# The recurrent passes stream both parts of x through one matmul of 512 columns, and the weights' rounding moves ahead of the gates

## The chip, the cores and the metric

The kernel runs on one core of a Trainium2 chip. The metric is the device time of one execution in microseconds; for the kernel before it is 1924.56, the median of three runs (1923.87 to 1925.30). The profiled execution took 1924.1 us by the same clock; its span, from the first to the last instruction of the trace, is 1922.0 us.

## The reference

The program computes three layers on x of 256 tokens by 2048 features, in fp32. The first layer holds the part that the change touches: RMS norm, one wide projection `z = xn @ w_in`, then a recurrent branch, an attention branch and gates. Cut to the recurrent branch:

```
xn = rms_norm(x, norm_pre_w)
u_lru, g_lru, ... = split(xn @ w_in)                 # 2048 features each
u = centred_depthwise_conv(u_lru, conv_w, conv_b)    # four taps along the tokens
for each direction (forward, backward):
    gate_r = sigmoid(u @ w_r + b_r); gate_i = sigmoid(u @ w_i + b_i)   # 16 blocks of 128
    a = exp(-8 * gate_r * softplus(-lam))
    h += scan over the tokens of  a * h + sqrt(1 - a*a) * (gate_i * u)
y_a = h * silu(g_lru)
```

Attention, the merging of both branches and two further layers of another kind follow; the change leaves them alone but for the value of some semaphore waits.

## The kernel before

**Slots.** All weights are cut into slots of 128 x 2048 fp32 values (1 MB) and pass through a ring of five places. For each slot SyncE issues a DMA (line 267) as soon as the slot five before it is used up; ScalarE rounds it to fp32r (`w_hi`, `Ring.round`, line 273); VectorE writes the remainder (`w_lo`, `Ring.residual`, line 281); TensorE then multiplies. x is split in the same way, into `xn_hi` and `xn_lo`, which lie side by side in one tile `xn`. A product is w_hi x_hi + w_hi x_lo + w_lo x_hi.

**Two ways to multiply a slot of features.** `Ring.features` (line 299) loads a 128 x 128 weight tile and streams 256 columns, three times for each of 16 tiles of the contraction, all into the same 256 columns of a PSUM bank: 48 matmuls per slot (line 308). `Ring.halves` (line 311) sends w_hi once against both parts of x as 512 columns and w_lo against x_hi as 256, so 32 matmuls per slot (lines 319 and 320); the sum then lies in two halves of the bank, and someone has to add them. The attention part of the kernel uses `halves` already, and there VectorE adds with a `tensor_reduce` (line 946).

**Passes.** The recurrent branch takes eight passes i of two feature tiles each (b = 0, 1). A pass has four slots: 4i and 4i+1 give u (banks z[0], z[1]), 4i+2 and 4i+3 give the gate g (banks z[2], z[3]). Then TensorE does 16 plain fp32 matmuls for the recurrent gates (`gates`, line 1126), which need the convolved u of this pass. TensorE runs its own instruction list pass by pass; each of the four slots waits until its bank was read out in the pass before.

**ScalarE and VectorE.** Both run a written-out order in nine iterations i (lines 616 to 644 and 880 to 910). Iteration i does the input side of pass i (copy of u out of PSUM, convolution) and the output side of pass i-1 (gates, decays, scan, y), and between these pieces the rounding and the remainder of slots n+3 to n+6, n = 4i. No engine reorders its list. In order, in the kernel before:

- ScalarE: sigmoid of g read from PSUM (`gate_inputs`, line 572), eight gate sigmoids (580, 582), round(n+3), four tanh (592), round(n+4), two copies of u into `padded` (610), four exp (599), a square root (602), round(n+5), round(n+6), rounding of y (614).
- VectorE: g times its sigmoid (`open_gates`, 850), residual(n+3), residual(n+4), two convolutions (839, 843), scan (856 to 865), residual(n+5), sum of directions and y (870, 873), residual(n+6), remainder of y (877).
- GpSimd multiplies gate_i by u (524).

In iteration 0 VectorE computes a softplus chain at the end (lines 912 to 917), and in iteration 2 a chain for the rotary tables (366 to 375), between y and residual(n+6). After the last pass come four slots for the keys (32 to 35, `tokens`, line 332) and four for the values (36 to 39); after slot 37 TensorE transposes the keys (1167), for which VectorE has rotated them (924 to 930).

Of the kernel before, what the change touches and what calls it, by code (L numbers as in the profile page):

```python
# [12 lines left out]
ACT = mybir.ActivationFunctionType  # L13
ALU = mybir.AluOpType
AX_X = mybir.AxisListType.X
# [3 lines left out]
T = 256  # L19
# [13 lines left out]
LRU_PASSES = KT // 2  # L33
# [326 lines left out]
def reduce_angles(link, dve, angle, turns, rest, looked):  # L360
# [4 lines left out]
    for n, quarter in enumerate((0.0, 0.25)):  # L365
# [5 lines left out]
        for m, part in enumerate(turn_parts):  # L371
# [3 lines left out]
        link(lambda: dve.tensor_scalar(rest, rest, -3.1415925, None, ALU.max))  # L375


B1_SEMS = ("loaded0 loaded1 loaded2 loaded3 loaded4 rounded split used "
           "p1_in ident_in consts_in x0 x1 x2 x3 eps squared averaged rooted first0 first1 first2 first_rounded first_split second_rounded second_split scaled ascaled turned xrounded xsplit "
           "weights0 weights1 gated cleared chain exped ucopied conv gsig zcopied gates taken decay dsteps rounded_y ydone "  # L380
           "counted rotary_in rchain rlooked mask_in sink_in sinkready "
# [6 lines left out]
def first_parts(k, t, s):  # L388

    nc = k.nc  # L390
    z, aux = k.z, k.aux
# [65 lines left out]
    def tile(n):  # L457
        return z[n][:, 0:T]
# [67 lines left out]
    def scalar(act):  # L526
# [38 lines left out]
        ring.round(act, 2)  # L565

        def gate_inputs(i):
            act.wait_ge(s.used, 4 * i + 4)
            if i:
                act.wait_ge(s.zcopied, 2 * i)  # L570
            for b in range(2):
                act.activation(gsig[:, b], tile(2 + b), ACT.Sigmoid).then_inc(s.gsig, 1)

        def gates(i):
            if i:
# [28 lines left out]
        def input_copy(i, b):  # L604
            act.wait_ge(s.used, 4 * i + b + 1)
            if i:
                act.wait_ge(s.conv, 8 * (i - 1) + 4 * b + 4)
            else:
                act.wait_ge(s.cleared, 1)
            act.activation(padded[:, b, 2:2 + T], tile(b), ACT.Copy).then_inc(s.ucopied, 1)  # L610

        def round_y(i):
            act.wait_ge(s.dsteps, 8 * i + 8)
# [1 line left out]

        for i in range(LRU_PASSES + 1):
            n = 4 * i
            if i:
                gate_inputs(i - 1)
                gates(i - 1)  # L620
            ring.round(act, n + 3)
            if i:
                tanhs(i - 1)
            ring.round(act, n + 4)
            if i < LRU_PASSES:
                input_copy(i, 0)
                input_copy(i, 1)
            if i:
                exps_lru(i - 1)
            else:  # L630
                act.wait_ge(s.chain, 2)
                act.activation(tmp[1][:], tmp[0][:], ACT.Exp).then_inc(s.exped, 1)
            ring.round(act, n + 5)
            if i == 2:

                act.wait_ge(s.rchain, RCHAIN_1 + 8)
                act.activation(sin_1[:, :, 0:16], rest_1[:, :, 0:16], ACT.Sin, scale=-1.0).then_inc(s.rlooked, 1)
                act.activation(sin_1[:, :, 16:32], rest_1[:, :, 16:32], ACT.Sin).then_inc(s.rlooked, 1)
            ring.round(act, n + 6)
            if i == 2:  # L640
                act.wait_ge(s.rchain, RCHAIN_1 + 16)
                act.activation(cos_1[:], rest_1[:], ACT.Sin).then_inc(s.rlooked, 1)
            if i:
                round_y(i - 1)
# [29 lines left out]
            act.activation(yb_hi[:, 4 * c + 2 * p:4 * c + 2 * p + 2], y_now[p][:], ACT.Copy).then_inc(yrounded[p], 1)  # L674

        def silu(c, j):
            act.wait_ge(s.zcopied, 2 * LRU_PASSES + 4 * c + j + 1)
            act.activation(gate[:, j], gate[:, j], ACT.Silu).then_inc(s.silued, 1)

        def finish_chunk(c, n):  # L680
# [102 lines left out]
    def vector(dve):  # L783
# [46 lines left out]
               .then_inc(s.second_split if q < 3 else s.split, 1)  # L830
        ring.residual(dve, 2)

        def convolve(i, b):
            dve.wait_ge(s.ucopied, 2 * i + b + 1)
            u = u_all[:, 2 * i + b:2 * i + b + 1]
            for tap in range(4):
                x = padded[:, b, tap:tap + T]
                if tap == 0:
                    ins = dve.tensor_scalar(u, x[:, None], col(P1_CONV, 2 * i + b), col(P1_CONVB, 2 * i + b),
                                            ALU.mult, ALU.add)  # L840
                else:
                    dve.wait_ge(s.conv, 8 * i + 4 * b + tap)
                    ins = dve.scalar_tensor_tensor(out=u, in0=x[:, None], scalar=col(P1_CONV + 16 * tap, 2 * i + b),
                                                   in1=u, op0=ALU.mult, op1=ALU.add)
                ins.then_inc(s.conv, 1)

        def open_gates(i):
            dve.wait_ge(s.gsig, 2 * i + 2)
            for b in range(2):
                dve.tensor_tensor(g_all[:, b], tile(2 + b), gsig[:, b], ALU.mult).then_inc(s.zcopied, 1)  # L850

        def scan(i):
            def step(n):
# [14 lines left out]
        def outputs_lru(i):  # L868
            dve.wait_ge(s.dsteps, 8 * i + 6)
            dve.tensor_tensor(gate_r[:, :, 0], gate_r[:, :, 0], gate_r[:, :, 1], ALU.add).then_inc(s.dsteps, 1)  # L870
            dve.wait_ge(s.zcopied, 2 * i + 2)
            dve.wait_ge(s.dsteps, 8 * i + 7)
            dve.tensor_tensor(y[:], gate_r[:, :, 0], g_all[:], ALU.mult).then_inc(s.dsteps, 1)

# [4 lines left out]

        for i in range(LRU_PASSES + 1):  # L880
            n = 4 * i
            if i:
                open_gates(i - 1)
            ring.residual(dve, n + 3)
            if i == 0:
                link = chain(dve, s.chain)
                link(lambda: dve.tensor_scalar(rate[:], params[:, P1_LAM:P1_LAM + 32], -1.0, None, ALU.mult))
                link(lambda: dve.tensor_tensor(tmp[0][:], rate[:], params[:, P1_LAM:P1_LAM + 32], ALU.min))
            ring.residual(dve, n + 4)
            if i < LRU_PASSES:  # L890
                convolve(i, 0)
                convolve(i, 1)
            if i:
                scan(i - 1)
            if i == 2:
                rlink = chain(dve, s.rchain)
                dve.wait_ge(s.counted, 1)
                dve.wait_ge(s.rotary_in, 16)
                rlink(lambda: dve.tensor_copy(angle_1[:], pos_1[:]))
                for m in range(2):  # L900
                    rlink(lambda: dve.tensor_tensor(angle_1[:, m], angle_1[:, m], rotary[:], ALU.mult))
            ring.residual(dve, n + 5)
            if i:
                outputs_lru(i - 1)
            if i == 2:
                reduce_angles(rlink, dve, angle_1[:], turns_1[:], rest_1[:], (s.rlooked, 2))
            ring.residual(dve, n + 6)
            if i:
                split_y(i - 1)
            else:  # L910
                dve.wait_ge(s.exped, 1)
                softplus_tail(link, dve, rate[:], tmp[1][:], tmp[0][:], tmp[2][:])
                link(lambda: dve.tensor_scalar(scale_a[:], rate[:], -8.0, None, ALU.mult))
                link(lambda: dve.tensor_scalar(scale_t[:], rate[:], 4.0, None, ALU.mult))
                dve.wait_ge(s.sink_in, 16)
                for b in range(2):
                    dve.tensor_copy(sinks[:, :, b], sink_row[:]).then_inc(s.sinkready, 1)
# [183 lines left out]
    def tensor(pe):  # L1101
# [42 lines left out]
        for i in range(LRU_PASSES):  # L1144
            for b in range(2):
                if i:
                    pe.wait_ge(s.ucopied, 2 * (i - 1) + b + 1)
                    ring.features(pe, 4 * i + b, tile(b), k.xn_hi, k.xn_lo)
                else:
                    ring.features(pe, b, tile(b), k.xn_hi, k.xn_lo, (first_rows, second_rows)[b], False)  # L1150
            for b in range(2):
                if i:
                    pe.wait_ge(s.zcopied, 2 * (i - 1) + b + 1)
                ring.features(pe, 4 * i + 2 + b, tile(2 + b), k.xn_hi, k.xn_lo)
            gates(i)

        pe.wait_ge(s.ucopied, 2 * LRU_PASSES)
# [10 lines left out]
                if h % 2:  # L1168
                    ins.then_inc(out_sem, 1)

        pe.wait_ge(s.zcopied, 2 * LRU_PASSES)
        for w in range(4):
            ring.tokens(pe, SLOT_V + w, w, pair(1), k.xn_hi, k.xn_lo)
            if w == 1:
# [40 lines left out]
        for c in range(4):  # L1215
# [7 lines left out]
            for j in range(4):  # L1223
                if c == 0 and j < 2:
                    pe.wait_ge(s.vcopied, 2)
                else:
                    pe.wait_ge(s.zcopied, 2 * LRU_PASSES + 4 * c + j - 1)
                ring.halves(pe, n + 4 + j, z[2 + j % 2], k.xn)
                if j == 0:
                    if c:  # L1230
# [10 lines left out]

        for c in range(4):
            if c == 1:
                pe.wait_ge(s.zcopied, 2 * LRU_PASSES + 16)
            elif c:
                pe.wait_ge(s.mlsig, 2 * (c - 1))
            for w in range(4):
# [78 lines left out]
    "xin added out_half stored weight_in")  # L1326

FIRST_COUNTS = {
    "rounded": 155, "split": 155, "used": 152, "p1_in": 16, "ident_in": 16,
    "consts_in": 32, "x0": 16, "x1": 16, "x2": 16, "x3": 16, "eps": 1, "squared": 4, "averaged": 1, "rooted": 2,  # L1330
    "first0": 16, "first1": 16, "first2": 16, "first_rounded": 3, "first_split": 3, "second_rounded": 3,
    "second_split": 3, "scaled": 6, "ascaled": 2, "turned": 16, "xrounded": 16, "xsplit": 16, "weights0": 64,
    "weights1": 64, "gated": 16, "cleared": 1, "chain": 26, "exped": 1, "ucopied": 16, "conv": 64, "gsig": 16,
    "zcopied": 32, "gates": 8, "taken": 64, "decay": 72, "dsteps": 64, "rounded_y": 8, "ydone": 8, "counted": 1,
    "rotary_in": 16, "rchain": 19, "rlooked": 3, "mask_in": 16, "sink_in": 16, "sinkready": 2, "kcopied": 2,
    "kroped": 8, "kturned": 2, "keyed": 2, "vcopied": 2, "qcopied": 8, "roped": 32, "qturned": 8, "qevac": 8,
    "scored0": 4, "scored1": 4, "soft0": 48, "soft1": 48, "exped0": 20, "exped1": 20, "flipped0": 4, "flipped1": 4,
# [1800 lines left out]
```

## Time and profile before

| | |
|---|---|
| median of three runs | 1924.56 us |
| profiled execution | 1924.1 us, span 1922.0 us |
| TensorE busy with matmuls | 1892.5 us, 98% of the span |
| VectorE busy | 1274.7 us, 66% |
| ScalarE busy | 1105.7 us, 58% |
| chain of waits that ended last | TensorE 96% of the span |
| recurrent passes on TensorE | from 15.45 to 230.54 us |

Busy time says how long an engine was at work, not whether anything waited for it. The chain of waits goes back from the last instruction to what released it, each time; it names the engine that set the time at each moment. The timeline lists the instructions of an engine in order; in brackets behind an instruction stands how long the engine stood idle before it and whose result ended that. An instruction's duration and the step from its start to the next one's differ slightly, since neighbours overlap.

### The profile page before, as it was taken

The page shows a single profiled execution, that of the slowest core. Times are in us where ns is not written, and L with a number is a line of the kernel's source. Part 1 is how long each engine was busy: PE and PEld are TensorE (multiplying, and loading weights), DVE is VectorE, ACT ScalarE, POOL GpSimd, SP SyncE. Part 2 cuts the span into 40 slices and gives each one's busy share as a digit, 9 for nine tenths or more (in the row PEclk, how much of TensorE's full clock was granted, in tenths as well). Part 3 has the DMA queues.
Part 4 walks back from the last instruction along what each step waited for, and adds up shares of the span by engine and source line. Part 5 has one row for each costly group of instructions (what it writes and reads, how often), then busy time and mean ns, then how long its engine had stood idle before and what let it go on. Part 6 is the DMA issues. An engine that isn't in the chain of part 4 may idle for free.

```text
span 1922.0 us, 31540 instructions
## 1 busy us (share of the span) xinstructions
PE 1892.5 (98%) x13480; PEld 1695.7 (88%) x13480; DVE 1274.7 (66%) x1785; ACT 1105.7 (58%) x1510; POOL 70.6 (4%) x66
## 2 busy tenths in 40 slices
PE   7999999999999999999899999999999999999998
PEld 7999988888888888888799999998889999999887
DVE  7778766655544434655689888754658988876453
ACT  7787755554533334434745688926465567893541
POOL 0111100000000000000000000100000000010000
PEclk9999999999999999999999999999999999999999
DMA  7455454444455555565464444322666444432263
GB/s 260 186 181 184 163 186 170 154 154 161 166 197 194 189 189 198 191 246 197 185 226 161 172 138 152 132 71 93 233 218 223 176 155 156 151 128 94 67 229 122
DMA packets 52267, 328.91 MB, mean 171 GB/s; under 512 B 7968, under 2 KB 9888, under 8 KB 14368
## 3 DMA queue, kind: packets, MB, share of 16 engines
q1 hardware_dynamic: 52128, 326.90, 47.7%
q8 instruction: 106, 1.74, 0.4%
q14 instruction: 33, 0.27, 0.0%
HBM read 320.59 MB, written 6.29 MB: 170 GB/s over the span
## 4 chain that ended last, share of the span: by engine, by line
PE 96%; ACT 2%; DVE 1%; issue 0%; DMA 0%; SPq 0%; ACTq 0%; DVEq 0%
PE z L308 39%; PE z L332 38%; PE z L319 3%; PE z L320 2%; PE aux L1134 1%; PE aux L2738 1%; PE z L356 1%; PE z L344 1%; PE aux L2640 1%; PE aux L1199 1%; PE aux L1182 1%; PE aux L2743 1%; PE aux L2602 1%; PE z L2627 1%; ACT w_hi L273 0%; PE aux L2822 0%
## 5 line engine op out<-in xcount | busy, mean ns | idle before, releaser
L281 DVE TENSOR_TENSOR w_lo<-w_raw,w_hi 128x2048 fp32r<-128x2048 f32 x274 | 631.5, 2307 | 359.5 <-ACT w_hi L273 358.7
L273 ACT ACTIVATE w_hi<-w_raw 128x2048 fp32r<-128x2048 f32 x286 | 546.5, 1915 | 410.3 <-DMA w_raw<-in_w_dram 410.1
L308 PE MATMUL z<-xn,w_hi 128*128 128x256 f32 x3712 | 693.0, 288 | 0.0
L308 PEld LDWEIGHTS z<-xn,w_hi 128*128 128x128 f32 x3712 | 579.0, 192 | 20.1 <-issue 16.5
L308 PE MATMUL z<-xn,w_lo 128*128 128x256 f32 x1856 | 524.8, 283 | 0.0
L308 PEld LDWEIGHTS z<-xn,w_lo 128*128 128x128 f32 x1856 | 355.4, 192 | 0.0
L332 PE MATMUL z<-w_hi,xn 128*128 128x512 f32 x1136 | 355.4, 391 | 0.0
L332 PEld LDWEIGHTS z<-w_hi,xn 128*128 128x128 f32 x1136 | 213.3, 188 | 44.2
L332 PE MATMUL z<-w_lo,xn 128*128 128x512 f32 x568 | 221.0, 389 | 0.0
L332 PE MATMUL z<-w_hi,y_hi 128*128 128x512 f32 x368 | 143.6, 390 | 0.0
L332 PE MATMUL z<-w_hi,y_lo 128*128 128x512 f32 x368 | 143.3, 389 | 0.0
L332 PE MATMUL z<-w_lo,y_hi 128*128 128x512 f32 x368 | 143.2, 389 | 0.0
L332 PEld LDWEIGHTS z<-w_lo,xn 128*128 128x128 f32 x568 | 106.7, 188 | 21.6
L2062 DVE SCALAR_TENSOR_TENSOR acc<-padded_b,params,acc 128x256 f32<-128x256 f32 x240 | 98.5, 477 | 0.0
L319 PE MATMUL z<-xn,w_hi 128*128 128x512 f32 x256 | 92.1, 402 | 0.0
L332 PEld LDWEIGHTS z<-w_hi,y_lo 128*128 128x128 f32 x368 | 69.1, 188 | 14.3
L332 PEld LDWEIGHTS z<-w_hi,y_hi 128*128 128x128 f32 x368 | 69.1, 188 | 14.2
L332 PEld LDWEIGHTS z<-w_lo,y_hi 128*128 128x128 f32 x368 | 69.1, 188 | 14.1
L2216 DVE SCALAR_TENSOR_TENSOR conv<-padded,params,conv 128x256 f32<-128x256 f32 x108 | 58.1, 538 | 30.9 <-ACT conv L1789 28.3
L308 PE MATMUL z<-raw_hi,w_hi 128*128 128x256 f32 x256 | 74.6, 291 | 0.3
L308 PE MATMUL z<-raw_lo,w_hi 128*128 128x256 f32 x256 | 72.7, 284 | 0.0
L308 PE MATMUL z<-raw_hi,w_lo 128*128 128x256 f32 x256 | 72.7, 284 | 0.0
(421 smaller groups left out, 2429.0 us busy)
## 6 DMA issues: line engine op xcount, KB each, us to landing
w_raw<-in_w_dram SPq DMA_DIRECT2D x287, 1024.0 KB, 4.8
gate_w<-in_lru_w_dram SPq DMA_DIRECT2D x8, 512.0 KB, 3.6
x_t<-state_dram SPq DMA_DIRECT2D x2, 2048.0 KB, 10.1
x_first<-in_x_dram SPq DMA_DIRECT2D x4, 512.0 KB, 6.5
x_t<-in_x_dram SPq DMA_DIRECT2D x1, 2048.0 KB, 11.3
state_dram<-x_t SPq DMA_DIRECT2D x2, 1024.0 KB, 5.2
pw<-in_pw_dram SPq DMA_DIRECT2D x2, 1024.0 KB, 6.7
state_dram<-x_t SPq DMA_DIRECT2D x8, 256.0 KB, 6.0
```

The source lines that it names most:

```text
L273: act.activation(self.k.w_hi[:, self.place(n)], self.k.w_raw[:, self.place(n)], ACT.Copy).then_inc(self.s.rounded, 1)
L281: dve.tensor_tensor(self.k.w_lo[:, at], self.k.w_raw[:, at], self.k.w_hi[:, at].bitcast(F32), ALU.subtract)\
L308: ins = pe.matmul(out, w[:, kk], x[:, kk], start=kk == 0 and j == 0, stop=kk == KT - 1 and j == 2)
L319: pe.matmul(bank[:, 0:2 * T].rearrange("p (b t) -> p b t", b=2), w_hi[:, kk], x[:, :, kk], start=kk == 0, stop=False)
L320: ins = pe.matmul(bank[:, 0:T], w_lo[:, kk], x[:, 0, kk], start=False, stop=kk == KT - 1)
L332: ins = pe.matmul(outs[m], x[:, row, t], w[:, kk], start=row == 0 and j == 0, stop=row == KT - 1 and j == 2)
L344: ins = pe.matmul(outs[m], x[:, row, t], w[:, kk], start=False, stop=row == KT - 1 and j == 2)
L356: ins = pe.matmul(outs[m], x[:, row, t], w[:, kk, 0:V_COLS], start=row == 0 and j == 0, stop=False)
L1134: ins = pe.matmul(aux[2 * b + d][:, g * T:g * T + T], gate_w[i % 2][:, b, 2 * d + g], u_all[:, 2 * i + b], start=True, stop=True)
L1182: ins = pe.matmul(aux[2 * p + h][:, b * T:b * T + T], q_turned[:, 2 * p + h, P * b:P * b + P], keys[:, c], start=True, stop=True)
L2062: dve.scalar_tensor_tensor(out=acc[:, b], in0=padded_b[:, b, n:n + T], scalar=col(w), in1=acc[:, b], op0=ALU.mult, op1=ALU.add).then_inc(s ...
L2216: dve.scalar_tensor_tensor(out=conv[:, i], in0=padded[:, i, tap:tap + T], scalar=col(w), in1=conv[:, i], op0=ALU.mult, op1=ALU.add).then_i ...
```

## The change

In the recurrent passes `features` becomes `halves` for all 32 slots. For u, ScalarE still copies one half of the bank (it now counts `uhalf`), and VectorE adds the other half in place (`sum_input`), ahead of each convolution. For g, VectorE adds the two halves with a `tensor_reduce` into `g_all` (`sum_gates`); ScalarE's sigmoid now reads `g_all` and waits for these sums, and `open_gates` multiplies in place. `zcopied` so counts four per pass in place of two. Besides, ScalarE does round(n+3) ahead of the gates' sigmoids, and VectorE does residual(n+3) ahead of `sum_gates` and `open_gates`. The core of the diff:

```
         def gate_inputs(i):
-            act.wait_ge(s.used, 4 * i + 4)
-            if i:
-                act.wait_ge(s.zcopied, 2 * i)
+            act.wait_ge(s.zcopied, 4 * i + 2)
             for b in range(2):
-                act.activation(gsig[:, b], tile(2 + b), ACT.Sigmoid).then_inc(s.gsig, 1)
+                act.activation(gsig[:, b], g_all[:, b], ACT.Sigmoid).then_inc(s.gsig, 1)
...
-            act.activation(padded[:, b, 2:2 + T], tile(b), ACT.Copy).then_inc(s.ucopied, 1)
+            act.activation(padded[:, b, 2:2 + T], tile(b), ACT.Copy).then_inc(s.uhalf, 1)
...
         for i in range(LRU_PASSES + 1):
             n = 4 * i
+            ring.round(act, n + 3)
             if i:
                 gate_inputs(i - 1)
                 gates(i - 1)
-            ring.round(act, n + 3)
-            if i:
                 tanhs(i - 1)
             ring.round(act, n + 4)
...
+        def sum_input(i, b):
+            dve.wait_ge(s.uhalf, 2 * i + b + 1)
+            there = padded[:, b, 2:2 + T]
+            dve.tensor_tensor(there, there, z[b][:, T:2 * T], ALU.add).then_inc(s.ucopied, 1)
+
...
+        def sum_gates(i):
+            dve.wait_ge(s.used, 4 * i + 4)
+            if i:
+                dve.wait_ge(s.dsteps, 8 * i)
+            for b in range(2):
+                dve.tensor_reduce(g_all[:, b], z[2 + b][:, 0:2 * T].rearrange("p (h t) -> p t h", h=2), AX_X, ALU.add).then_inc(s.zcopied, 1)
+
         def open_gates(i):
             dve.wait_ge(s.gsig, 2 * i + 2)
             for b in range(2):
-                dve.tensor_tensor(g_all[:, b], tile(2 + b), gsig[:, b], ALU.mult).then_inc(s.zcopied, 1)
+                dve.wait_ge(s.zcopied, 4 * i + b + 1)
+                dve.tensor_tensor(g_all[:, b], g_all[:, b], gsig[:, b], ALU.mult).then_inc(s.zcopied, 1)
...
         for i in range(LRU_PASSES + 1):
             n = 4 * i
+            ring.residual(dve, n + 3)
             if i:
+                sum_gates(i - 1)
                 open_gates(i - 1)
-            ring.residual(dve, n + 3)
...
             if i < LRU_PASSES:
+                sum_input(i, 0)
                 convolve(i, 0)
+                sum_input(i, 1)
                 convolve(i, 1)
...
                 if i:
                     pe.wait_ge(s.ucopied, 2 * (i - 1) + b + 1)
-                    ring.features(pe, 4 * i + b, tile(b), k.xn_hi, k.xn_lo)
+                    ring.halves(pe, 4 * i + b, z[b], k.xn)
...
                 if i:
-                    pe.wait_ge(s.zcopied, 2 * (i - 1) + b + 1)
-                ring.features(pe, 4 * i + 2 + b, tile(2 + b), k.xn_hi, k.xn_lo)
+                    pe.wait_ge(s.zcopied, 4 * (i - 1) + b + 1)
+                ring.halves(pe, 4 * i + 2 + b, z[2 + b], k.xn)
```

Later waits on `zcopied` and the totals of the semaphores follow the new count.

## Rows read from the trace of the kernel before

**Rows 1.** Chain of waits, passes 6 and 7: start us, us, engine and line
```profile
200.60 3.46 PE aux L1134 x16
204.06 23.03 PE z L308 x192
...
230.54 32.69 PE z L332 x144
```

**Rows 2.** Timeline of TensorE in attention's `halves`: start us, us, instruction
```profile
298.03 0.40 PE L319 MATMUL z<-xn,w_hi 128*128 128x512 f32 x1
...
301.21 0.40 PE L319 MATMUL z<-xn,w_hi 128*128 128x512 f32 x1
...
303.84 0.39 PE L319 MATMUL z<-xn,w_hi 128*128 128x512 f32 x1
...
306.62 0.39 PE L319 MATMUL z<-xn,w_hi 128*128 128x512 f32 x1
```

**Rows 3.** Timeline of ScalarE, iteration 6 and the start of 7
```profile
178.44 0.63 ACT L614 ACTIVATE y_hi<-y 128x512 fp32r<-128x512 f32 x1 [5.03 <-DVE y L873]
...
180.39 0.66 ACT L572 ACTIVATE gsig<-z 128x256 f32<-128x256 f32 x2
...
183.79 1.99 ACT L273 ACTIVATE w_hi<-w_raw 128x2048 fp32r<-128x2048 f32 x1
185.59 1.76 ACT L592 ACTIVATE tau<-gate_r,scale_t 128x256 f32<-128x256 f32 x4
...
194.04 1.06 ACT L602 ACTIVATE tau<-tau 128x1024 f32<-128x1024 f32 x1
...
203.74 0.63 ACT L614 ACTIVATE y_hi<-y 128x512 fp32r<-128x512 f32 x1 [5.02 <-DVE y L873]
```

**Rows 4.** Timeline of VectorE, the same iteration
```profile
178.33 2.28 DVE L281 TENSOR_TENSOR w_lo<-w_raw,w_hi 128x2048 fp32r<-128x2048 f32 x1
180.53 0.68 DVE L877 TENSOR_TENSOR y_lo<-y,y_hi 128x512 fp32r<-128x512 f32 x1
181.13 0.74 DVE L850 TENSOR_TENSOR g_all<-z,gsig 128x256 f32<-128x256 f32 x2
...
189.19 2.29 DVE L281 TENSOR_TENSOR w_lo<-w_raw,w_hi 128x2048 fp32r<-128x2048 f32 x1 [0.43 <-ACT w_hi L273]
...
195.17 1.22 DVE L856 SCALAR_TENSOR_TENSOR tau<-decay,tau 128x1024 f32<-128x1024 f32 x1
```

**Rows 5.** Instructions of two lines over the whole span: ns min/median/max
```profile
L946 DVE TENSOR_REDUCE gate<-z x16: 680/685/692, 308.0 to 485.0; 128x256 f32<-128x512 f32 x16
...
L850 DVE TENSOR_TENSOR g_all<-z,gsig x16: 411/414/417, 47.6 to 233.0; 128x256 f32<-128x256 f32 x16
```

**Rows 6.** Timeline of VectorE, start of iteration 1
```profile
47.61 0.74 DVE L850 TENSOR_TENSOR g_all<-z,gsig 128x256 f32<-128x256 f32 x2
```

**Rows 7.** Timeline of VectorE, iteration 2, around the rotary chain
```profile
88.99 1.23 DVE L856 SCALAR_TENSOR_TENSOR tau<-decay,tau 128x1024 f32<-128x1024 f32 x1 [1.11 <-ACT tau L602]
...
102.42 2.29 DVE L281 TENSOR_TENSOR w_lo<-w_raw,w_hi 128x2048 fp32r<-128x2048 f32 x1
```

**Rows 8.** Timelines of ScalarE and VectorE, iteration 8; last, the chain of waits
```profile
231.93 0.66 ACT L572 ACTIVATE gsig<-z 128x256 f32<-128x256 f32 x2
...
246.14 1.23 DVE L856 SCALAR_TENSOR_TENSOR tau<-decay,tau 128x1024 f32<-128x1024 f32 x1 [3.11 <-ACT tau L602]
...
251.01 2.27 DVE L281 TENSOR_TENSOR w_lo<-w_raw,w_hi 128x2048 fp32r<-128x2048 f32 x1
...
258.79 0.29 DVE L930 TENSOR_TENSOR q_tok<-rope_a,rope_b 128x128 f32<-128x128 f32 x1
...
263.24 0.87 PE aux L1167 x8
```

**Rows 9.** TensorE between layers: timeline, then windows (PEclk third from last)
```profile
933.00 1.06 PE L2516 MATMUL aux<-ident,x_t 128*128 128x128 f32 x8 [3.64 <-DVE x_t L2007]
...
934.00:936.00 2.00, 1.14 (x6) 1.10 (x6) 1.17 (x4) 2.00 (x7) 0.00 (x0) 0.58 0.02 6
```

More of the change, by code:

```diff
@@ L375, in reduce_angles @@
         link(lambda: dve.tensor_scalar(rest, rest, -3.1415925, None, ALU.max))
-B1_SEMS = ("loaded0 loaded1 loaded2 loaded3 loaded4 rounded split used "
+B1_SEMS = ("uhalf loaded0 loaded1 loaded2 loaded3 loaded4 rounded split used "
            "p1_in ident_in consts_in x0 x1 x2 x3 eps squared averaged rooted first0 first1 first2 first_rounded first_split second_rounded second_split scaled ascaled turned xrounded xsplit "
@@ L676, in silu @@
         def silu(c, j):
-            act.wait_ge(s.zcopied, 2 * LRU_PASSES + 4 * c + j + 1)
+            act.wait_ge(s.zcopied, 4 * LRU_PASSES + 4 * c + j + 1)
             act.activation(gate[:, j], gate[:, j], ACT.Silu).then_inc(s.silued, 1)
@@ L870, in outputs_lru @@
             dve.tensor_tensor(gate_r[:, :, 0], gate_r[:, :, 0], gate_r[:, :, 1], ALU.add).then_inc(s.dsteps, 1)
-            dve.wait_ge(s.zcopied, 2 * i + 2)
+            dve.wait_ge(s.zcopied, 4 * i + 4)
             dve.wait_ge(s.dsteps, 8 * i + 7)
@@ L1147, in tensor @@
                     pe.wait_ge(s.ucopied, 2 * (i - 1) + b + 1)
-                    ring.features(pe, 4 * i + b, tile(b), k.xn_hi, k.xn_lo)
+                    ring.halves(pe, 4 * i + b, z[b], k.xn)
                 else:
-                    ring.features(pe, b, tile(b), k.xn_hi, k.xn_lo, (first_rows, second_rows)[b], False)
+                    ring.halves(pe, b, z[b], k.xn, (first_rows, second_rows)[b], False)
             for b in range(2):
                 if i:
-                    pe.wait_ge(s.zcopied, 2 * (i - 1) + b + 1)
-                ring.features(pe, 4 * i + 2 + b, tile(2 + b), k.xn_hi, k.xn_lo)
+                    pe.wait_ge(s.zcopied, 4 * (i - 1) + b + 1)
+                ring.halves(pe, 4 * i + 2 + b, z[2 + b], k.xn)
             gates(i)
@@ L1169, in turn_heads @@
                     ins.then_inc(out_sem, 1)
-        pe.wait_ge(s.zcopied, 2 * LRU_PASSES)
+        pe.wait_ge(s.zcopied, 4 * LRU_PASSES)
         for w in range(4):
@@ L1226, in tensor @@
                 else:
-                    pe.wait_ge(s.zcopied, 2 * LRU_PASSES + 4 * c + j - 1)
+                    pe.wait_ge(s.zcopied, 4 * LRU_PASSES + 4 * c + j - 1)
                 ring.halves(pe, n + 4 + j, z[2 + j % 2], k.xn)
@@ L1243, in tensor @@
             if c == 1:
-                pe.wait_ge(s.zcopied, 2 * LRU_PASSES + 16)
+                pe.wait_ge(s.zcopied, 4 * LRU_PASSES + 16)
             elif c:
@@ L1328 @@
 FIRST_COUNTS = {
+    "uhalf": 16,
     "rounded": 155, "split": 155, "used": 152, "p1_in": 16, "ident_in": 16,
@@ L1333 @@
     "weights1": 64, "gated": 16, "cleared": 1, "chain": 26, "exped": 1, "ucopied": 16, "conv": 64, "gsig": 16,
-    "zcopied": 32, "gates": 8, "taken": 64, "decay": 72, "dsteps": 64, "rounded_y": 8, "ydone": 8, "counted": 1,
+    "zcopied": 48, "gates": 8, "taken": 64, "decay": 72, "dsteps": 64, "rounded_y": 8, "ydone": 8, "counted": 1,
     "rotary_in": 16, "rchain": 19, "rlooked": 3, "mask_in": 16, "sink_in": 16, "sinkready": 2, "kcopied": 2,
```

## The prediction

> **What bounds the kernel now.** I read the chain of waits first. In passes 6 and 7 it holds nothing but TensorE: 16 gate matmuls in 3.46 us, then 192 matmuls in 23.03 us, then the keys' and values' slots from 230.54 [rows 1]. A pass is thus 26.49 us, and a k-tile of three 256-column matmuls takes 23.03/64 = 0.360 us. So anything that shortens TensorE's stream shortens the kernel, as long as the others keep up.
>
> Whether they do is read from the timelines of ScalarE and VectorE. These two run a ring of their own, with one turn per iteration. I start it at Y, the end of VectorE's y multiply, at which ScalarE's rounding of y starts: 178.44 in iteration 5, 203.74 in iteration 6 [rows 3]. A turn is 25.30 us, 1.19 less than TensorE's pass. The convolved u of pass 6 was ready when the scan started, at 195.17 [rows 4], and TensorE wanted it at 200.60 [rows 1]: 5.4 us to spare. TensorE is the bound, but the ring is close behind it, and every us put into the ring beyond 1.2 us per turn turns it into the bound. The share of busy time (VectorE 66%) doesn't show this; the turn does, since much of it is one engine waiting for the other.
>
> **What TensorE saves.** In attention a pair of 512 and 256 columns takes (301.21-298.03)/9 = 0.353 us in some slots and (306.62-303.84)/8 = 0.348 in others [rows 2]. Per k-tile 6.5 or 12.3 ns are saved; for 32 slots of 16 k-tiles that is 3.3 or 6.3 us, and a pass becomes 64 x 0.353 + 3.46 = 26.1 us, or 25.7. That is all the change can bring. The Trainium skill (TensorE: Matmul & The Clock Gate, Wait — 56ns, not 53.3ns?) puts back-to-back matmuls at N/2.4 GHz plus about 2.5 ns each; by that one matmul less per k-tile would save 2.5 ns, 1.3 us in all. Here the 256-column matmul steps by 120 ns, more than that rule's 109, so the rows decide.
>
> **What the ring gets.** Two new kinds of work on VectorE, and one new wait.
>
> (a) `sum_input`: two additions of 256 elements per pass, one operand in PSUM, the form of the g multiply at 414 ns [rows 5]. With the wait of the next instruction 0.45 each, 0.90 us, straight ahead of the convolutions. Bounds: 0.33 (step between neighbours without a wait) to 0.50 each.
>
> (b) `sum_gates`: two reduces of the form of attention's, 685 ns each, steps of 0.60 [rows 5]: the first ends 0.68 after its start, the second 1.28.
>
> (c) The new wait: the sigmoid of g waits for both sums, and these stand behind residual(n+6), the remainder of y and residual(n+3) on VectorE. Behind the sigmoid, ScalarE queues eight gate sigmoids, four tanh and round(n+4), for which VectorE then waits.
>
> (d) The moved round(n+3) takes 185.59-183.79 = 1.80 us out of that ScalarE stretch [rows 3] and is done while VectorE is still busy. Its data are there: the slot was freed in the middle of the pass before. The moved residual(n+3) loses its old wait for ScalarE, but that time wasn't spare; it becomes the wait of residual(n+4).
>
> The new turn, from Y: in the old one, VectorE was through with residual(n+6) and the remainder of y at 181.13, Y+2.69 [rows 3, 4]. Now residual(n+3) follows, a step of 2.20 (180.53-178.33) [rows 4], to Y+4.89. The first sum ends at Y+5.57, the second at Y+6.17, so the sigmoid starts at Y+6.2 where it started at Y+1.95 (180.39) [rows 3]. From the sigmoid to residual(n+4) it was 189.19-180.39 = 8.80; without the 1.80 it is 7.00: residual(n+4) at Y+13.2 instead of Y+10.75. To the scan's start it was 195.17-189.19 = 5.98, now 6.88 with (a): conv done at Y+20.08. ScalarE's square root, which the scan needs too, ends 14.71-1.80 = 12.9 after the sigmoid [rows 3], Y+19.1, just not the later one. Scan to next Y as before, 203.74-195.17 = 8.57. **Turn: 28.65 us** instead of 25.30, against TensorE's 25.7 to 26.1. The ring becomes the bound, and TensorE's saving turns into waiting, some 2.6 us a pass.
>
> **The start and the end of the ring.** Iteration 1: VectorE comes out of the softplus at 47.61 [rows 6], now 48.51 because of (a). Residual(7) to 50.71, both sums at 51.99, sigmoid at 52.0, residual(8) at 59.0, conv(1) done at 65.9, Y2 = 74.45. TensorE asked for conv(1) at 200.60 - 5 x 26.49 = 68.15 [rows 1], now 1 us or so earlier: no wait yet. Conv(2) is done at 74.45+20.08 = 94.5; TensorE asked at 94.6, now 1.3 to 2.3 earlier: it waits that long and stands level with the old time.
>
> Iteration 2 carries the rotary chain. From the scan's start to residual(n+6) it took 102.42-88.99 = 13.43 [rows 7]. Normally it is 8.57 less the 178.44-178.33 = 0.11 by which residual(n+6) starts ahead of Y [rows 3, 4], 8.46: 4.97 more. So Y3 = 74.45+28.65+4.98 = 108.1. In pass 3 TensorE wants bank z[2] at 94.5 + 3.46 + two slots of 5.6 = 109.2 and gets it at Y3+5.57 = 113.7. It waits again for conv(3), done at 128.2, 7.1 later than it asked for it before (200.60 - 3 x 26.49).
>
> From there one turn per pass: Y7 = 108.1 + 4 x 28.65 = 222.7, conv(7) 242.8, gates 3.46, keys' slots from 246.25 instead of 230.54 [rows 1]: **+15.7 us**.
>
> Iteration 8 has no convolution. Y8 = 251.35, sigmoid at 257.55. Before, from sigmoid to scan 246.14-231.93 = 14.21 [rows 8], now 12.41: scan at 269.96. Residual(37) starts 4.87 later (251.01-246.14) [rows 8], at 274.8, and ends at 277.1. TensorE, with 32.69/144 = 0.227 us per matmul [rows 1] and 24 per slot, would like slot 37 at 246.25 + 5 x 5.45 = 273.5. It waits 3.6 us, where it had 4.5 to spare (230.54+27.25 against 251.01+2.27). Slot 37 ends at 282.55; the rotated keys are ready 12.94 after the scan's start (258.79+0.29-246.14) [rows 8], at 282.9. The transposes so start at 282.9 instead of 263.24: **+19.7 us**.
>
> Behind that TensorE is again the bound; ScalarE and VectorE have only rounding to do ahead, and nothing later gives time back. The changed waits on `zcopied` there ask for the same events.
>
> The profiled execution would take 1924.1 + 19.7 = 1943.8; the median of the runs lies 0.5 above it, so **1944.3 us**. Uncertain are the terms that recur: 0.2 us in a turn is 1.4 us in the sum, and (a) by its bounds moves the turn by -0.24 to +0.10, -1.7 to +0.7 us in seven turns. The pace of the pairs doesn't enter. Own range 1941 to 1947.
>
> **Rivals.** Each is a mechanism of its own.
>
> The clock falls. After 3.64 us without work TensorE ran at a granted 0.58 in the next window of 2 us, a mix of its levels 1.2 and 2.4 GHz [rows 9]. The new kernel makes it wait once per pass, 2 to 5 us each. In the passes this costs nothing: a stretch at half clock loses about 2 us at most (0.84 us in that row, doubled as my choice), and there are 2.6 to spare per turn. Behind the wait at slot 37 no spare is left: plus 1 to 3 us, 1945 to 1947. Against it: 2.8 us may be too short a pause. The Trainium skill (TensorE: Matmul & The Clock Gate, Why this matters for your kernels) warns of idle gaps between bursts, after which the clock halves; by that rule this rival would be the case, and the change bad for that reason too. The trace agrees for the one long gap between the layers.
>
> The sigmoid doesn't hold the ring up. If something I read as serial runs beside it, only (a) remains: a turn of 26.2, at TensorE's pace. The lag of iteration 2 would still cost 2 us or so against 3 to 6 saved: 1922 to 1927. For it speaks only that ScalarE stood idle 5.03 us before Y [rows 3]; but that pause lies behind the chain, not in it.
>
> Faster: TensorE's stream alone sets the end, as it does now, and the kernel gains the pairs' 3.3 to 6.3 us: 1918 to 1921. It needs a turn of under 26.0, 2.65 us below my sum, with the first bank sum early enough. As VectorE's additions are priced by rows of the same form, and the old turn comes out of the same rows, I see nothing that could give this.
>
> **How the numbers follow.** Forecast 0.67, clock 0.25, no hold-up 0.03, faster 0.05. About 0.2% (3.8 us) is what a measurement of this kernel can tell from no change. Forecast and clock are slower, 0.92; the third is mostly within 0.2%, 0.03; faster 0.05. Range 1939 to 1949: the first two cases with a little more error in the turn than its terms suggest.
>
> **What would show it.** In the profile after: ScalarE's rounding of y recurs every 28.65 us from pass 3 on; g's sigmoid stands idle before it until a reduce of VectorE; VectorE waits over 4 us for w_hi at residual(n+4) and not at residual(n+3); TensorE's gate matmuls each wait 2 to 3.5 us for line 843, and a slot of pass 3 waits about 4.5 for a reduce; slot 37 waits 3.6 for w_lo; the keys' slots start near 246. If the turn is 26 or less, or the gate matmuls don't wait, the forecast is wrong. If the turn is right but the end is off, the error is in the ends of the ring.

## The result, and the profile after

The changed kernel takes 1947.71 us (median of four runs, 1947.60 to 1947.88) against 1924.21 for the kernel before: a ratio of 1.012, 95% interval 1.0108 to 1.0132. It is 23.5 us slower. The forecast was 1944.3, the range 1939 to 1949, so the measured time lies inside it.

The chain that ended last, of the changed kernel, by engine and by line:

```profile
PE 83%; DVE 10%; ACT 5%; issue 1%; DMA 0%; SPq 0%; DVEq 0%; ACTq 0%
PE z L332 36%; PE z L308 29%; DVE w_lo L281 4%; PE z L319 3%; PE z L320 2%; PE aux L2752 1%; ACT w_hi L273 1%; PE z L356 1%; DVE u_all L845 1%; PE z L344 1%; PE aux L2654 1%; PE aux L1195 1%; PE aux L1212 1%; ACT gate_i L580 1%; ACT gate_r L578 1%
```

TensorE had 96% of it before. Its busy share is 98% in both kernels: busy time doesn't show that the bound moved to other engines in one part of the program. One turn of the new chain (start us, us, what; the view lists the longest pieces only), from the remainders behind y of one iteration to the y of the next:

```profile
224.93 2.20 DVE w_lo L281
227.65 2.28 DVE w_lo L281
229.93 1.21 DVE g_all L854 x2
235.25 1.30 ACT tau L590 x3
236.55 1.81 ACT w_hi L273
238.39 2.29 DVE w_lo L281
...
245.28 1.23 DVE tau L866
...
250.23 2.18 DVE w_lo L281
...
253.12 0.69 DVE y L883
```

TensorE is not in this turn. It holds VectorE's residual(n+6) and residual(n+3), its two gate sums, ScalarE's tanh and rounding, VectorE's residual(n+4), scan, y. This answers to the pure TensorE chain of [rows 1].

The same ring (ScalarE and VectorE, each waiting for the other once per iteration) in the timeline of ScalarE, iteration 6 of the changed kernel, against [rows 3]:

```profile
196.08 0.64 ACT L612 ACTIVATE y_hi<-y 128x512 fp32r<-128x512 f32 x1 [5.97 <-DVE y L883]
196.62 1.90 ACT L273 ACTIVATE w_hi<-w_raw 128x2048 fp32r<-128x2048 f32 x1
198.54 1.28 ACT L570 ACT_TABLE_LOAD   x1
202.29 0.72 ACT L570 ACTIVATE gsig<-g_all 128x256 f32<-128x256 f32 x2 [2.47 <-DVE g_all L854]
...
205.41 0.51 ACT L580 ACTIVATE gate_i<-aux,params 128x256 f32<-128x256 f32 x1
205.95 1.71 ACT L590 ACTIVATE tau<-gate_r,scale_t 128x256 f32<-128x256 f32 x4
...
224.96 0.64 ACT L612 ACTIVATE y_hi<-y 128x512 fp32r<-128x512 f32 x1 [5.97 <-DVE y L883]
```

and in that of VectorE, against [rows 4]:

```profile
198.77 2.28 DVE L281 TENSOR_TENSOR w_lo<-w_raw,w_hi 128x2048 fp32r<-128x2048 f32 x1
200.97 1.28 DVE L854 TENSOR_REDUCE g_all<-z 128x256 f32<-128x512 f32 x2
...
209.50 2.29 DVE L281 TENSOR_TENSOR w_lo<-w_raw,w_hi 128x2048 fp32r<-128x2048 f32 x1 [5.69 <-ACT w_hi L273]
211.71 0.41 DVE L833 TENSOR_TENSOR padded<-padded,z 128x256 f32<-128x256 f32 x1
...
216.40 1.22 DVE L866 SCALAR_TENSOR_TENSOR tau<-decay,tau 128x1024 f32<-128x1024 f32 x1
```

With Y = 196.08 (Y is the start of ScalarE's rounding of y) the sigmoid starts at Y+6.21 after standing idle 2.47 us for VectorE's sums; residual(n+4) starts at Y+13.42, after VectorE stood idle 5.69 us for the rounding; the scan starts at Y+20.32, and the next Y is 28.88 later. The turn was 25.30.

What TensorE waits for in the recurrent passes (its timeline, idle time and releaser in brackets):

```profile
96.00 1.22 PE L1147 MATMUL aux<-u_all,gate_w 128*128 128x256 f32 x3 [2.44 <-DVE u_all L845]
...
115.04 0.50 PE L319 MATMUL z<-xn,w_hi 128*128 128x512 f32 x1 [2.54 <-DVE g_all L854]
...
129.88 1.39 PE L1147 MATMUL aux<-u_all,gate_w 128*128 128x256 f32 x4 [3.47 <-DVE u_all L845]
...
158.77 1.56 PE L1147 MATMUL aux<-u_all,gate_w 128*128 128x256 f32 x6 [0.88 <-DVE u_all L845]
...
187.65 0.70 PE L1147 MATMUL aux<-u_all,gate_w 128*128 128x256 f32 x2 [2.97 <-DVE u_all L845]
...
216.54 3.72 PE L1147 MATMUL aux<-u_all,gate_w 128*128 128x256 f32 x16 [1.28 <-DVE u_all L845]
...
245.42 3.02 PE L1147 MATMUL aux<-u_all,gate_w 128*128 128x256 f32 x9 [2.55 <-DVE u_all L845]
...
279.85 0.50 PE L332 MATMUL z<-w_hi,xn 128*128 128x512 f32 x1 [1.80 <-DVE w_lo L281]
```

Six groups of gate matmuls wait for the convolution, 13.6 us in all; one slot of pass 3 waits for a gate sum, and slot 37 for its remainder. The end of the stretch, from the chain, and the windows view of TensorE behind three of the waits (granted clock third from last):

```profile
279.85 7.35 PE z L332 x24
287.20 0.88 PE aux L1180 x8
```

```profile
96.00:98.00 2.00, 2.00 (x6) 1.63 (x7) 1.97 (x2) 1.95 (x2) 0.00 (x0) 0.62 0.03 8
...
159.00:161.00 2.00, 2.00 (x10) 1.77 (x10) 1.97 (x2) 2.00 (x2) 0.00 (x0) 1.00 0.00 0
...
280.00:282.00 2.00, 2.00 (x7) 1.58 (x8) 1.90 (x3) 0.77 (x2) 0.00 (x0) 0.70 0.99 418
```

The keys' transposes start at 287.20 instead of 263.24 [rows 8], 23.96 us later; the whole span grew by 1946.1 - 1922.0 = 24.1. So nearly all of the loss lies ahead of that point. Slot 37 took 7.35 us for 24 matmuls that take 5.45 in an unbroken stream; behind 280:282 with its 0.70, the next windows of 2 us read 0.50 and 0.95.

### The profile page after: what moved, and what is told of

Read it like the earlier page. It is cut to its first block, busy times and chain, and to the rows that moved or that the text cites. A ratio compares the mean times of both kernels' runs of the same rounds, so it can differ in the third digit from the quotient of the medians.

```text
span 1946.1 us, 30556 instructions
## 1 busy us (share of the span) xinstructions
PE 1898.5 (98%) x12968; PEld 1673.6 (86%) x12968; DVE 1285.4 (66%) x1817; ACT 1106.5 (57%) x1510; POOL 70.5 (4%) x66
## 4 chain that ended last, share of the span: by engine, by line
PE 83%; DVE 10%; ACT 5%; issue 1%; DMA 0%; SPq 0%; DVEq 0%; ACTq 0%
PE z L332 36%; PE z L308 29%; DVE w_lo L281 4%; PE z L319 3%; PE z L320 2%; PE aux L2752 1%; ACT w_hi L273 1%; PE z L356 1%; DVE u_all L845 1%; PE z L344 1%; PE aux L2654 1%; PE aux L1195 1%; PE aux L1212 1%; ACT gate_i L580 1%; ACT gate_r L578 1%
## 5 line engine op out<-in xcount | busy, mean ns | idle before, releaser
L308 PE MATMUL z<-xn,w_hi 128*128 128x256 f32 x2688 | 505.2, 289 | 0.0
L308 PEld LDWEIGHTS z<-xn,w_hi 128*128 128x128 f32 x2688 | 418.8, 191 | 19.5 <-issue 16.5
L308 PE MATMUL z<-xn,w_lo 128*128 128x256 f32 x1344 | 379.8, 283 | 0.0
L319 PE MATMUL z<-xn,w_hi 128*128 128x512 f32 x768 | 275.4, 402 | 2.5 <-DVE g_all L854 2.5
L308 PEld LDWEIGHTS z<-xn,w_lo 128*128 128x128 f32 x1344 | 257.1, 191 | 0.0
L320 PE MATMUL z<-xn,w_lo 128*128 128x256 f32 x768 | 214.9, 280 | 0.0
L319 PEld LDWEIGHTS z<-xn,w_hi 128*128 128x128 f32 x768 | 144.6, 188 | 36.2 <-DVE g_all L854 2.9
L320 PEld LDWEIGHTS z<-xn,w_lo 128*128 128x128 f32 x768 | 145.3, 189 | 0.5
```

The lines of the kernel that those rows point to most:

```text
L308: ins = pe.matmul(out, w[:, kk], x[:, kk], start=kk == 0 and j == 0, stop=kk == KT - 1 and j == 2)
L319: pe.matmul(bank[:, 0:2 * T].rearrange("p (b t) -> p b t", b=2), w_hi[:, kk], x[:, :, kk], start=kk == 0, stop=False)
L320: ins = pe.matmul(bank[:, 0:T], w_lo[:, kk], x[:, 0, kk], start=False, stop=kk == KT - 1)
```

## The experiments

The theory: ScalarE and VectorE form a ring whose turn bounds the passes, and the gate sums and the additions lengthen it. Rival A: the moved rounding is what costs. Rival B: TensorE itself got slower, and the ring only follows. Times are medians; ratios are against runs of the kernel before on the same chip. That kernel's median is 1925.07 us beside e1 to e4 and 1924.62 beside e5 to e8, against 1924.21 beside the changed kernel, so a difference from the changed kernel can be off by up to 0.9 us.

**e1_order_alone.** The kernel before, with the order alone changed (and the same on ScalarE):

```
             n = 4 * i
+            ring.residual(dve, n + 3)
             if i:
                 open_gates(i - 1)
-            ring.residual(dve, n + 3)
```

> The kernel before with only the order changed: ScalarE's round(n+3) ahead of the sigmoids, VectorE's residual(n+3) ahead of open_gates; 256-column matmuls and no sums. Theory (the turn of ScalarE and VectorE, 28.9 us in the changed kernel, bounds it, because VectorE's sums stand ahead of the sigmoid): the turn stays near 25.4, under TensorE's 26.5, so no difference from before, 1923 to 1926. Rival A (the moved rounding is what costs): most of the 23.5 us shows here, 1940 or more.

Measured: 1924.91, ratio 0.9998 (0.9989 to 1.0007). The rounding of y recurs every 25.45 us (153.73, 179.18), and TensorE waits nowhere in the passes. The move alone costs nothing; rival A falls.

**e2_sums_old_order.** The changed kernel with the old order on both engines:

```
             n = 4 * i
-            ring.residual(dve, n + 3)
             if i:
                 sum_gates(i - 1)
                 open_gates(i - 1)
+            ring.residual(dve, n + 3)
```

> The changed kernel with the order of before put back: the sums come right behind the remainder of y, round(n+3) and residual(n+3) behind the gates. Theory: the sigmoid starts 4.0 us after Y, residual(n+4) 8.9 later, a turn of 28.3 instead of 28.9, so 4 us faster than the changed kernel, 1942 to 1945. Rival A: all of the loss goes away, 1919 to 1924.

Measured: 1942.18, ratio 1.0087 (1.0072 to 1.0103). Y recurs every 28.32 us (164.55, 192.87). The move makes the loss 5.5 us larger once the sums are there, for the sigmoid then stands behind one remainder more. That is a little more than the 4 expected: the turns give 3.4 (six at 0.57), and the first and the last iteration 1.0 and 0.5 more. Most of the loss stays without the move.

**e4_ring_alone.** The ring of the changed kernel, the TensorE stream of before. u and g come out doubled:

```
-                    ring.halves(pe, 4 * i + b, z[b], k.xn)
+                    ring.features(pe, 4 * i + b, tile(b), k.xn_hi, k.xn_lo)
...
-            dve.tensor_tensor(there, there, z[b][:, T:2 * T], ALU.add).then_inc(s.ucopied, 1)
+            dve.tensor_tensor(there, there, tile(b), ALU.add).then_inc(s.ucopied, 1)
...
-                dve.tensor_reduce(g_all[:, b], z[2 + b][:, 0:2 * T].rearrange("p (h t) -> p t h", h=2), AX_X, ALU.add)...
+                dve.tensor_reduce(g_all[:, b], tile(2 + b)[:, :, None].to_broadcast([P, T, 2]), AX_X, ALU.add)...
```

> The changed kernel's ScalarE and VectorE lists, but TensorE streams three times 256 columns as before; the sums add the first half of the bank twice, so u and g come out doubled. Theory: TensorE's pace doesn't enter where the ring bounds: 1946 to 1949, as the changed kernel, with the same turn of 28.9. Rival B: TensorE is back to its old stream, so the time falls to 1924 to 1930.

Measured: 1947.91, ratio 1.0118 (1.0105 to 1.0132), as the changed kernel. Rival B falls: with the old stream of 256-column matmuls on TensorE, none of the loss comes back. Its ScalarE timeline has the same ring:

```profile
195.88 0.63 ACT L612 ACTIVATE y_hi<-y 128x512 fp32r<-128x512 f32 x1 [5.97 <-DVE y L883]
...
224.77 0.63 ACT L612 ACTIVATE y_hi<-y 128x512 fp32r<-128x512 f32 x1 [5.97 <-DVE y L883]
```

The turn is 28.89 us here too.

**e5_u_without_sum.** u's slots by 256 columns, no additions, g as changed:

```
-                    ring.halves(pe, 4 * i + b, z[b], k.xn)
+                    ring.features(pe, 4 * i + b, tile(b), k.xn_hi, k.xn_lo)
...
-                sum_input(i, 0)
                 convolve(i, 0)
-                sum_input(i, 1)
                 convolve(i, 1)
```

> The changed kernel, but u's two slots per pass are streamed as three times 256 columns and ScalarE's copy suffices, so VectorE's two additions per pass are gone; g keeps the pairs and the sums. Theory (the turn is a sum of terms on one chain; the additions are 0.45 each): turn 28.0 instead of 28.9, 6 to 7 us faster than the changed kernel, 1940 to 1943. Rival (VectorE's additions lie beside the wait for the square root and cost less): 1944 or more.

Measured: 1941.15, ratio 1.0088 (1.0074 to 1.0101), 6.6 us faster than the changed kernel. Y recurs every 27.97 us (190.81, 218.78), 0.92 less: the two additions cost the turn their full price, and seven turns of it are 6.4 us.

**e3_sums_behind_y.** The changed kernel, the gate sums taken right behind y, where TensorE has long filled the banks:

```
-                sum_gates(i - 1)
                 open_gates(i - 1)
...
                 outputs_lru(i - 1)
+                if i < LRU_PASSES:
+                    sum_gates(i)
...
             else:
+                sum_gates(0)
                 dve.wait_ge(s.exped, 1)
```

> The changed kernel with one move: VectorE sums the gate banks of pass i right behind y of pass i-1 (in iteration 0 ahead of the softplus), so the sigmoid never waits for residual(n+3). The same instructions otherwise. Theory: sigmoid 3.7 us after Y, residual(n+4) at 10.9, a turn of 26.3 instead of 28.9, close to TensorE's 25.7 to 26.1; the waits of TensorE go away but for the rotary chain's, and the pairs' gain shows: 1918 to 1923. Rival B (TensorE itself is slower with pairs and at a fallen clock, the ring only follows it): little changes, 1943 to 1948.

Measured: 1926.64, ratio 1.0009 (1.0000 to 1.0018). The same instructions as in the changed kernel, 21 us faster, but not in the expected 1918 to 1923. The turn is 26.43 (157.04, 183.47), 0.13 over the sum, and stays above TensorE's pass. The rotary chain in iteration 2 costs the ring 32.84 - 26.43 = 6.41 us (71.34, 104.18) and nothing wins it back. TensorE waited 3.19 us for it:

```profile
122.18 3.34 PE L1149 MATMUL aux<-u_all,gate_w 128*128 128x256 f32 x9 [3.19 <-DVE u_all L845]
```

It ran on at a granted clock of 0.78, 0.50 and 0.87 in the windows 122:124 to 126:128, came up with the ring again by pass 7 (a wait of 0.53 at 227.92), and waited 1.05 at slot 37. I had left the chain and the longer turn out of the number though the text of the expectation named the chain. A third part is missing from that text: two steps of the softplus, slowed beside GpSimd (rows in the last section), lie on the chain of waits and set the ring back by 2.1 us before its first turn.

**e6_ring_relieved and e8_rotary_in_2.** Two more moves, not separated from each other: VectorE reduces u from PSUM itself, in the idle time ahead of residual(n+4), with the first convolution behind it, and ScalarE's copy goes; in e6 the rotary chain also moves from iteration 2 to 6. Against e3:

```
-            there = padded[:, b, 2:2 + T]
-            dve.tensor_tensor(there, there, z[b][:, T:2 * T], ALU.add).then_inc(s.ucopied, 1)
+            dve.tensor_reduce(padded[:, b, 2:2 + T], z[b][:, 0:2 * T].rearrange("p (h t) -> p t h", h=2), AX_X, ALU.add).then_inc(s.ucopied, 1)
...
-            ring.residual(dve, n + 4)
             if i < LRU_PASSES:
                 sum_input(i, 0)
                 convolve(i, 0)
                 sum_input(i, 1)
+            ring.residual(dve, n + 4)
+            if i < LRU_PASSES:
                 convolve(i, 1)
```

> The changed kernel with three moves: gate sums right behind y; u summed by a tensor_reduce of VectorE straight from PSUM, without ScalarE's copy, and with the first convolution placed ahead of residual(n+4), where VectorE stood idle; the rotary chain in iteration 6 instead of 2. Theory: turn under 25.5, TensorE the bound again, no wait of the gate matmuls; the pairs' gain of 3.3 to 6.3 us shows: 1918 to 1921. Rival: pairs bring nothing in the passes, 1924 or more.

Measured: 1920.11, ratio 0.9977 (0.9967 to 0.9986), inside the expected range, but with one wait left, of 0.78 us at slot 37.

> e6_ring_relieved with the rotary chain left in iteration 2. Theory: the ring lags 6.4 us once, with about 5 us to spare in pass 3; TensorE waits 0 to 2 us at the gate matmuls of pass 3 and nowhere else: 0 to 3 us over e6. Rival (the place of the chain is what made the gain): as the kernel with the sums behind y, 1926.

Measured: 1918.85, ratio 0.9970 (0.9957 to 0.9982): faster than the kernel before, by 5.8 us. It isn't behind e6 but 1.3 ahead, so the chain's place in iteration 6 was a loss: too near the end, it left slot 37 a wait of 0.78 us and 5.74 us instead of 5.45. The ring's turn is 24.94 us (177.30, 202.22), and TensorE waits nowhere in the passes. Its chain of waits has TensorE alone there, as in [rows 1]:

```profile
66.88 3.45 PE aux L1150 x16
...
92.94 3.45 PE aux L1150 x16
118.58 3.45 PE aux L1150 x16
...
144.22 3.45 PE aux L1150 x16
...
225.03 32.68 PE z L332 x144
```

Passes of 26.06, 25.64 and 25.64 us where it was 26.49, and the keys' slots at 225.03 instead of 230.54.

**e7_ring_relieved_256.** e6 with three times 256 columns, the reduces reading the first half twice, as in e4.

> As the run before, but TensorE streams three times 256 columns, and VectorE's reduces read the first half twice (u and g come out doubled). Theory: TensorE's stream is the bound in both, so this one takes the time of the kernel before, 1923 to 1926, and the difference to the run before is the pairs' gain alone.

Measured: 1924.84, ratio 1.0001 (0.9992 to 1.0010). Between e7 and e6 only TensorE's stream differs: 4.7 us, within the forecast 3.3 to 6.3. That is what is left of the pairs' gain after the 1.1 us that e6, and not e7, loses at slot 37 (0.78 and 0.29); my estimate of the pairs alone is the sum, 5.8.

## Why the prediction was right, and where 3.8 us went missing

The forecast loss was 19.7 us (1944.3 against 1924.56), the measured one is 23.5, so 3.8 us more. The range that was stated, 1939 to 1949, holds; the "own range" of the sum, 1941 to 1947, is missed by 0.7.

**The bound.** The ring takes over, as forecast: the chain shows it, and e4 shows that TensorE's pace has no say.

**The terms.** Against the working in the prediction:

| | forecast | measured |
|---|---|---|
| sigmoid behind Y | 6.2 | 6.21 |
| sigmoid to residual(n+4) | 7.00 | 7.21 |
| residual(n+4) to scan | 6.88 | 6.90 |
| turn | 28.65 | 28.89 |
| additions in a turn | 0.90 | 0.92 (e5) |
| Y2 | 74.45 | 75.55 |
| Y8 | 251.35 | 253.84 |
| wait at slot 37 | 3.6 | 1.80 |
| slot 37 | 5.45 | 7.35 |
| keys' transposes | 282.9 | 287.20 |

Forecast and measured start of the transposes are 4.3 us apart. They are made up of: 1.1 from the start; 1.4 from six turns at 0.23 more; 0.2 more from the sigmoid to the scan in iteration 8; and 1.55 from slot 37, which took 1.90 more, less the 0.35 that the transposes would have waited. Of the 1.90, 0.29 comes with a wait as such: in e3 and e6 slot 37 takes 5.74 us behind a wait of 1.05 and 0.78 while the granted clock stays at 1.00. The other 1.6 is the fallen clock. (The 4.3 are counted in the trace; in the profiled execution the loss is 1947.88 - 1924.1 = 23.8 against 19.7, and between the medians 23.5.)

The ScalarE stretch was forecast 0.21 too short, since I took the old step through a row of other work. The first tanh now starts 0.54 after the last gate sigmoid (205.95 - 205.41), where each step before it is 0.36; in the old order round(n+3) lay between and started after 0.36. The experiments agree: 0.57 in e1, which has the new order, and 0.36 in e2, which has the old one. The pair of sigmoids of g, which now reads SBUF, takes 0.08 more up to the next start (0.63 against 0.55 from PSUM), and round(n+4) gives 0.07 back up to the remainder.

The start, 1.1 us: 0.84 of it is there when residual(7) starts, at 49.35 against 48.51. The first pass interleaves the slot with the transposes of x, and two of these take 0.63 us rather than 0.38 for longer: until 17.99, against 16.60 before. The pairs are not the main reason, for e4 with the old stream has the slow steps until 17.83 and starts residual(7) at 49.19, 0.68 late. Runs with the old stream start their first gates anywhere between 41.7 and 42.6. What sets it stays open.

**The rivals.** The clock case, with its chance of 0.25, was told as an alternative to the forecast; it happened on top of it. Granted were 0.62 behind the wait of 2.44 us and 0.70 behind that of 1.80. My reason against it, that 2.8 us may be too short, was wrong. The Trainium skill (TensorE: Matmul & The Clock Gate, Why this matters for your kernels) warns of idle gaps between bursts of matmuls; the trace agrees that the clock falls behind them, here behind shorter ones than the page names. Its price in the passes was nothing, as said, since the ring bounds there. It explains why TensorE's waits are not the forecast 2 to 3.5 us each, but 0.88 to 3.47: at the fallen clock 16 gate matmuls take 5.41 us instead of 3.62, which comes off the next wait. It also explains the shorter wait at slot 37, since TensorE needed 32.6 us from 245.42 until it asked for that slot, instead of 30.7. The slot of pass 3 waited 2.54 instead of 4.5 us for its bank: TensorE came 3.3 us later than forecast (112.5), 1.5 by the later convolution and 1.8 by the clock, and the bank 1.3 later (115.04). The faster case and the case without a hold-up are refuted by the turn; the pairs' gain that the faster case counted on exists (e7 to e6), but only where the ring keeps up.

**Which part costs what.** The additions 6.6 us (e5), the move of the rounding 5.5 (e2) although it is free without the sums (e1), and the place of the gate sums 21 (e3). These overlap and don't add up: each is read against the changed kernel.

## What to carry to other kernels

Before giving work to an engine that is two thirds busy, measure the turn of the loop that it forms with its neighbours: here 25.3 us against the bound's 26.5, so 1.2 us were free and 3.6 were added. Where an added step stands in the order can matter more than its size. Here the same sums cost 21 us more ahead of the sigmoid than right behind y, where the other engine had work of its own: there the turn is 26.43 (e3), which is e1's 25.45, 0.92 for the additions and 0.06 left for the gate sums. A place in which an engine stands idle in every turn is where a new step belongs, if its data are there by then.

## What the hardware showed that I had not expected

The pairs run at one of two paces for a whole pass, 25.64 or 26.06 us with the gates (e8: two of the seven passes from the first gates to the last are slow, with two fast ones between them); 64 pairs at 0.347 and 0.353 us, and the gates' 3.45, give just these. What chooses is open.

In the changed kernel the granted clock fell behind waits of 2.44, 2.55, 2.97, 3.47 and even 1.80 us, and did not behind one of 2.54 (115.04, ahead of a slot), 1.28 or 0.88. In e5 it fell behind one of 2.52 at the same slot (granted 0.71, then 0.50). The length of one wait alone doesn't tell.

VectorE slows while GpSimd multiplies. In e8 a convolution's first tap takes three times its usual 0.41 us, when it falls beside the multiply of gate_i (timeline of VectorE):

```profile
209.89 1.24 DVE L841 TENSOR_SCALAR u_all<-padded,params 128x256 f32<-128x256 f32 x1
...
216.33 0.41 DVE L841 TENSOR_SCALAR u_all<-padded,params 128x256 f32<-128x256 f32 x1
```

In e3 the same happened to small steps of the softplus beside GpSimd's 2.54 us:

```profile
48.78 2.54 POOL L524 TENSOR_TENSOR gate_i<-gate_i,u_all 128x512 f32<-128x512 f32 x2 [47.74 <-ACT gate_i L580]
```

```profile
48.62 0.19 DVE L172 TENSOR_TENSOR tmp<-tmp,tmp 128x32 f32<-128x32 f32 x1
48.84 1.27 DVE L173 TENSOR_SCALAR tmp<-tmp 128x32 f32<-128x32 f32 x1
50.14 1.22 DVE L174 TENSOR_TENSOR tmp<-tmp,tmp 128x32 f32<-128x32 f32 x1
```

A step of 0.18 us becomes 1.27, about the length of one of the two multiplies. In the changed kernel the multiply falls into VectorE's idle time (206.00 to 208.54 in the iteration shown), so this has no part in the loss.
